# Eight modulation chunks moved from the WKV stage into the feed-forward stage, four of them on VectorE

## The chip, the cores and the metric

One Trainium2 chip, one of its cores. The metric is the device time of one execution in microseconds; the kernel before has a median of 1135.08 us over 3 runs (1134.55 to 1142.41). Lower is better.

## The reference, cut to what matters

Two blocks follow each other on 256 tokens of width 1024. The first block is a mixer (an attention branch and an RWKV-7 branch, merged under gates) and a gated feed-forward network of width 2816. The second is a state-space mixer and a mixture of 32 experts. What the change moves belongs to the second block but needs nothing of the first: the modulation, a product of one row with a matrix.

```python
# second_block; c is (1, 1024), w_ada is (1024, 6144)
mod = jax.nn.silu(c) @ w_ada[layer] + b_ada[layer]
sh1, sc1, g1, sh2, sc2, g2 = jnp.split(mod, 6, axis=-1)
h = modulate(x, sh1, sc1)          # first use: the input of the second block
...
x = x + g1[:, None, :] * mix
# first_block, the stage that receives the work
f = (jax.nn.silu(h @ w_ffn_gate[l]) * (h @ w_ffn_up[l])) @ w_ffn_down[l]
```

## The kernel before, in words

The program is written out by hand, one instruction stream for each engine, joined by semaphores. Each stream is executed in the order in which it is written, the DMA-issuing stream of SyncE (SP) among them.

**Weights.** All weights up to the experts pass through a ring of three slots of 4096 words per partition (2 MB each). The list `W` gives their order. SP walks it: before it fills a slot it waits (`consumed`) until the last matmul on the slot's former content is done. The keys that matter here: `("gate", 0..3)`, `("ada", c)` for the 512-column chunks of `w_ada`, and `("ff", 0..10)`, each of which holds 256 columns of `w_ffn_gate` and 256 of `w_ffn_up` (two DMAs of 1 MB). The content of most slots is split into a rounded high part (ScalarE, `high_parts`, L1645, two instructions of 128x2048) and a remainder (VectorE, `low_parts`, L558, two more); the matmuls are then three per product (`by_parts`, L767 to L769).

**PSUM.** `plan_banks` lists all uses of the eight banks in PE's order; use n goes to bank n mod 8 and waits until use n-8 has been drained (`write`, `drained`, `free`).

**One modulation chunk**, before: PE multiplies the chunk's eight k-tiles (128x512) by the broadcast column of silu(c), as four column tiles of 32 that run side by side (`ada_chunk`, L933); ScalarE copies the bank to `modp` (`ada_rows`, L1759); PE sums the four parts over the partitions with a constant (`ada_sum`, L911 into columns for chunks 0 to 3, L914 over rows for the gates 4, 5, 10, 11); VectorE adds the bias (`ada_sum`, L2316, L2319). Eight chunks, `ADA_EARLY`, are done in the WKV stage: `ada(turn)` stands between its steps and does the sum of the last chunk and the product of the next. Four others, `ADA_LATE`, are done in the second block and are not touched.

**The WKV stage** (146 to 220 us) inverts triangular 64x64 blocks level by level. At each of the levels 1 to 5, PE computes four groups `x` (L1018), which ScalarE copies (L1776); then, after `ada(lv + 1)`, four pairs of groups `d` and `dt` (L1018 too), which VectorE merges (L2345, L2347), and from these come the `x` of the next level. The chunks' DMAs, and those of gate 1 to 3, are `PACED`: a quarter at a time, each behind an event of the stage.

**The feed-forward stage** (317 to 442 us): 22 tiles f of 128 columns. PE makes gate and up of a tile in one bank (48 matmuls), ScalarE takes the silu (L1833), VectorE multiplies (L2451), and after each odd f ScalarE copies the pair's high part (L1838). Also after each odd f, both split slot `("ff", f // 2 + 3)`: the slot that SP requested when PE had finished this same f. The normed input `xn1`, in the arena, is dead once its transposes `("hT", 1, kk)` are drained.

Of the kernel before, what the change touches and what calls it, by code (L numbers as in the profile page):

```python
# [167 lines left out]
def ada_banks(turn):  # L168

    return ([("as", ADA_EARLY[turn - 1])] if turn else []) + ([("ad", ADA_EARLY[turn])] if turn < len(ADA_EARLY) else [])  # L170


def plan_banks():
# [32 lines left out]
    o += [("ff", m) for m in range(KF)]  # L206
# [21 lines left out]
ADA_EARLY = (0, 1, 2, 3, 4, 5, 10, 11)  # L228
ADA_LATE = (6, 7, 8, 9)
# [19 lines left out]
    ("modp", 2 * 512, TOKENS, GATES), ("gm", NT * HEADS * 4 * CH, WKV, WKV), ("dd", NT * HEADS * CH, WKV, WKV),  # L249
# [43 lines left out]
    "osb": 28672, "kk": 28672, "fpost": 28672, "ysq": 28672, "one": 28672, "acT": 29184, "modp": 29696, "xn1": 29696,  # L293
# [18 lines left out]
def build(nc, A, out):  # L312
    BANK = plan_banks()
    ctx = ExitStack()
    with ctx:
# [56 lines left out]
        def B(name, *dims):  # L372
# [6 lines left out]
            if len(dims) == 3:  # L379
# [14 lines left out]
        modp = {c: (junk[:, 512 * (c % 2):512 * (c % 2) + 512] if c in ADA_LATE else B("modp", 2)[:, c % 2])  # L394
                for c in ADA_EARLY + ADA_LATE}
# [83 lines left out]

        for c in ADA_EARLY:  # L480
            modulation(c)
# [24 lines left out]

        def level_paces(lv):
            nxt = ("x", 1, lv + 1, 0) if lv < LEVELS - 1 else ("w1", 1, 0)
            return ("dt", 0, lv, 1), ("dt", 1, lv, 1), nxt

        PACED = {("ada", ADA_EARLY[3]): (("g", 0, 0, 0), ("g", 0, 1, 0), ("g", 1, 0, 0)),
                 ("ada", ADA_EARLY[4]): (("n", 0, 0), ("n", 1, 0), ("x", 0, 1, 0)),
                 ("ada", ADA_EARLY[5]): level_paces(1), ("ada", ADA_EARLY[6]): level_paces(2),
                 ("ada", ADA_EARLY[7]): level_paces(3), ("gate", 1): level_paces(4), ("gate", 2): level_paces(5),
# [192 lines left out]
        def _(pe):  # L707
# [209 lines left out]
            def ada(turn):  # L917

                if turn:
                    ada_sum(ADA_EARLY[turn - 1])  # L920
# [1963 lines left out]
```

## Time and profile before

| what | us |
|---|---|
| median of 3 runs | 1135.08 |
| the profiled execution | 1133.99 |
| its span, first to last instruction | 1132.1 |
| mean granted TensorE clock | 0.991 of 2.4 GHz |
| WKV stage (from the first gram to the head means) | 145 to 219 |
| feed-forward tiles on PE | 317 to 442 |
| experts | from about 670 |

The table's stages are read from the timeline. Time outside the span is 1.9 us, and the profiled execution is 1.1 us under the median, so a difference of a few us counts from 1134.0.

### The profile page before, as it was taken

How to read it: one execution, taken by the hardware profiler on the slowest of the kernel's cores; microseconds unless marked ns; L12 is line 12 of the kernel's file. 1: busy time of each engine (PE TensorE's matmuls, PEld its weight loads, DVE VectorE, ACT ScalarE, POOL GpSimd, SP SyncE). 2: the span in 40 equal slices, each digit the busy share in tenths (PEclk: the TensorE clock that was granted, in tenths of full speed). 3: DMA queues.
4: the chain of work that ended last, by engine and by line, in shares of the span. 5: the costliest groups of instructions: out<-in, count | busy, mean ns of one | idle time of the engine just before them, and what ended most of it. 6: DMA issues, size and time to landing. Idle time of an engine off the chain costs nothing.

```text
span 1132.1 us, 17911 instructions
## 1 busy us (share of the span) xinstructions
PE 1058.2 (93%) x7545; PEld 720.2 (64%) x7545; DVE 461.8 (41%) x698; ACT 354.1 (31%) x508; POOL 39.5 (3%) x32
## 2 busy tenths in 40 slices
PE   5999999999999999999999999999899989898986
PEld 4997877799789999877986453444244433242432
DVE  4784244367655353557648351222122212121212
ACT  4752322364454343455543220111011111010102
POOL 0001310001000101000000000000000000000000
PEclk9999999999999999999989999999999999999999
DMA  9444377434545655463465869999999999999994
GB/s 318 147 174 159 135 236 238 139 145 173 187 130 183 190 186 186 186 219 130 167 224 209 363 257 421 419 419 421 420 421 421 420 421 421 421 420 421 420 420 191
DMA packets 95445, 316.31 MB, mean 279 GB/s; under 512 B 8262, under 2 KB 33174, under 8 KB 70678
## 3 DMA queue, kind: packets, MB, share of 16 engines
q1 hardware_dynamic: 94342, 312.70, 72.1%
q10 hardware_dynamic: 1040, 2.69, 0.7%
q8 instruction: 50, 0.82, 0.3%
q14 instruction: 13, 0.11, 0.0%
HBM read 314.32 MB, written 1.05 MB: 279 GB/s over the span
## 4 chain that ended last, share of the span: by engine, by line
PE 72%; DMA 21%; DVE 4%; ACT 2%; issue 1%; SPq 0%; POOL 0%; DVEq 0%; ACTq 0%
DMA arena<-in_w 20%; PE bank L1474 11%; PE bank L767 11%; PE bank L769 11%; PE bank L768 11%; PE bank L1498 4%; PE bank L753 4%; PE bank L1018 3%; PE bank L933 2%; PE bank L1454 1%; PE bank L967 1%; PE bank L744 1%; PE bank L1511 1%; PE bank L714 1%; DVE arena L2560 1%
## 5 line engine op out<-in xcount | busy, mean ns | idle before, releaser
L1474 PE MATMUL bank<-ring,hT 128*64 128x512 f32 x512 | 227.0, 595 | 29.8 <-DMA arena<-in_w 28.6
L1474 PE MATMUL bank<-arena,hT 128*64 128x512 f32 x512 | 227.0, 595 | 0.0
L769 PE MATMUL bank<-h_high,ring_low 128*128 128x256 f32 x688 | 193.8, 282 | 0.0
L1474 PEld LDWEIGHTS bank<-ring,hT 128*64 128x64 f32 x512 | 67.8, 137 | 182.2 <-issue 130.2
L558 DVE TENSOR_TENSOR ring_low<-ring,hi_high 128x2048 fp32r<-128x2048 f32 (+2 forms) x58 | 126.0, 2218 | 100.8 <-ACT hi_high L1645 100.8
L767 PE MATMUL bank<-h_high,hi_high 128*128 128x256 f32 x528 | 148.1, 280 | 0.0
L768 PE MATMUL bank<-h_low,hi_high 128*128 128x256 f32 x528 | 147.5, 279 | 0.0
L1645 ACT ACTIVATE hi_high<-ring 128x2048 fp32r<-128x2048 f32 (+2 forms) x58 | 104.5, 1854 | 92.0 <-DMA ring<-in_w_ffn_up 33.9
L769 PEld LDWEIGHTS bank<-h_high,ring_low 128*128 128x128 f32 x688 | 130.8, 190 | 0.0
L1498 PE MATMUL bank<-arena 128*64 128x512 f32 x384 | 113.3, 595 | 7.1 <-DVE hT L2772 6.7
L2778 DVE TENSOR_TENSOR arena<-arena,bank 128x512 f32<-128x512 f32 x16 | 17.4, 1084 | 231.0 <-ACT arena L2002 231.0
L767 PEld LDWEIGHTS bank<-h_high,hi_high 128*128 128x128 f32 x528 | 99.4, 188 | 1.1 <-issue 1.0
L768 PEld LDWEIGHTS bank<-h_low,hi_high 128*128 128x128 f32 x528 | 99.8, 189 | 0.1
L2002 ACT ACTIVATE arena<-bank 128x512 f32<-128x512 f32 x16 | 9.6, 598 | 232.8 <-PE bank L1474 232.8
L1474 PEld LDWEIGHTS bank<-arena,hT 128*64 128x64 f32 x512 | 67.8, 137 | 0.0
L1498 PEld LDWEIGHTS bank<-arena 128*64 128x64 f32 x384 | 35.1, 137 | 40.5 <-issue 39.4
L1498 PE MATMUL bank<-ring,arena 128*64 128x512 f32 x128 | 56.6, 595 | 4.3 <-ACT arena L2006 4.3
L2011 ACT ACTIVATE y_high<-con 128x512 fp32r<-128x512 f32 x32 | 20.2, 630 | 125.1 <-DVE con L2792 125.1
L2792 DVE SCALAR_TENSOR_TENSOR con<-bank,small,arena 128x512 f32<-128x512 f32 x32 | 24.0, 751 | 86.3 <-PE bank L1498 86.3
L767 PE MATMUL bank<-h_high,hrw_high 128*128 128x256 f32 x160 | 46.5, 291 | 0.7 <-DVE ring_low L558 0.7
L768 PE MATMUL bank<-h_low,hrw_high 128*128 128x256 f32 x160 | 45.9, 287 | 0.0
L1498 PEld LDWEIGHTS bank<-ring,arena 128*64 128x64 f32 x128 | 16.9, 137 | 37.7 <-issue 36.1
(401 smaller groups left out, 1706.7 us busy)
## 6 DMA issues: line engine op xcount, KB each, us to landing
arena<-in_w SPq DMA_DIRECT2D x112, 1024.0 KB, 23.0
ring<-in_w SPq DMA_DIRECT2D x80, 1024.0 KB, 20.5
ring<-in_w_in SPq DMA_DIRECT2D x12, 2048.0 KB, 7.8
ring<-in_w_ada SPq DMA_DIRECT2D x7, 2048.0 KB, 8.2
ring<-in_w_ffn_gate SPq DMA_DIRECT2D x11, 1024.0 KB, 5.5
ring<-in_w_ffn_up SPq DMA_DIRECT2D x11, 1024.0 KB, 8.2
ring<-in_w_ada SPq DMA_DIRECT2D x20, 512.0 KB, 5.0
ring<-in_w_ffn_down SPq DMA_DIRECT2D x5, 2048.0 KB, 7.9
```

The source lines that it names most:

```text
L558: return eng.tensor_tensor(ring_lo[:, r, c0:c1], ring[:, r, c0:c1], high_of(n)[:, c0:c1].bitcast(F32), ALU.subtract)
L753: last = mm(ps[:, 0:512], lhs[k][:, i * P:(i + 1) * P], w[:, k, 0:512], start=(k == 0), stop=(k == nk - 1))
L767: mm(ps, a[0], b[0], start=start, stop=False)
L768: mm(ps, a[0], b[1], start=False, stop=False)
L769: return mm(ps, a[1], b[0], start=False, stop=stop)
L933: last = mm(ps[32 * j:32 * j + 32, 0:512], cb[:, k, :], w[:, k, :], start=(kk == 0), stop=(kk == 1))
L1018: last = mm(ps[r, j * w:(j + 1) * w], left(4 * q + j, r), right(4 * q + j, r), start=True, stop=True)
L1474: last = mm(both(6 + half, x), hg[:, k, (2 * q + x) * CAP:(2 * q + x + 1) * CAP], w13s[x][k // 4][:, k % 4, half * EF:(half + 1) * EF], st ...
L1498: last = mm(both(4 + n, x), acT[:, 0, f, x * CAP:(x + 1) * CAP], w2s[q][x][f // 2][:, f % 2, n * 512:(n + 1) * 512], start=(f == 0), stop= ...
L1645: A_(high_of(n)[:, f], ring[:, r, f], ACT.Copy).then_inc(S("high"), 1)
L2011: A_(y_hi[n], y_out[:, n, :], ACT.Copy).then_inc(S("y_high"), 1)
L2792: V.scalar_tensor_tensor(y_out[:, n, :], bank[4 + n][:, :], slot_gate[:, 0:1], g2[:, n * 512:(n + 1) * 512], ALU.mult, ALU.mult).then_inc( ...
```

## The change

The eight early chunks leave the ring's list, the WKV stage and its banks. Gate 1 to 3 follow gate 0 directly and are loaded whole. The third and fourth attention output (`("o", 2)`) gets two idle matmuls (`keep_busy`) in place of `ada(0)`.

In the feed-forward stage, chunk t of the eight is tied to tiles f = 2t+2 and 2t+3. SP loads it in two halves of four k-tiles (1 MB) into one buffer, `ada_half`, which is the dead `xn1`: after slot `("ff", t + 3)` the first half, once the chunk before is consumed; then a wait for `half_used`; then the second half; only then slot `("ff", t + 4)`. Odd t go through PE as before, one half after each tile (`ada_part`), with the row copy on ScalarE ahead of its slot split. Even t (`ADA_DVE`) go through VectorE: per k-tile one product that accumulates in `modp` (`ada_products`, four after each tile, ahead of the slot split), and PE sums over the partitions with a constant of minus ones, which the bias addition takes back as a subtraction. The column sums of chunk t-1 stand behind tile 2t+3.

```diff
-    ("modp", 2 * 512, TOKENS, GATES), ("gm", ...
+    ("gm", ...
+ADA_DVE = ADA_EARLY[0::2]
+    for f in range(KF):
+        t = f // 2 - 1
+        o += [("ff", f)] + ([("as", ADA_EARLY[t - 1])] if f % 2 and 0 < t <= len(ADA_EARLY) else [])
+        o += [("ad", ADA_EARLY[t])] if f % 2 == 0 and 0 <= t < len(ADA_EARLY) and ADA_EARLY[t] not in ADA_DVE else []
+        ada_half = B("xn1").rearrange("p (k c) -> p k c", k=KD // 2)
@@ SP
-        for c in ADA_EARLY:
-            modulation(c)
-                if key == ("ada", 3):
+                if key == ("gate", 2):
...
+                if key[0] == "ff" and 3 <= key[1] < 3 + len(ADA_EARLY):
+                    c = ADA_EARLY[key[1] - 3]
+                    src = cols(A["w_ada_2"][0], c * 512, c * 512 + 512)
+                    if key[1] == 3:
+                        drained(sp, ("hT", 1, 3))
+                    elif ADA_EARLY[key[1] - 4] in ADA_DVE:
+                        sp.wait_ge(S("ada_acc"), ADA_DVE.index(ADA_EARLY[key[1] - 4]) + 1)
+                    else:
+                        filled(sp, ("ad", ADA_EARLY[key[1] - 4]))
+                    sp.dma_start(ada_half, src[:, 0:4, :]).then_inc(S("half_full"), 16)
+                    sp.wait_ge(S("half_used"), key[1] - 2)
+                    sp.dma_start(ada_half, src[:, 4:8, :]).then_inc(S("half_full"), 16)
@@ PE
                 if p == 2:
-                    ada(0)
+                    keep_busy(write(pe, ("o", p)), 2)
...
-                ada(lv + 1)
...
+            def ada_part(t, part):
+                c = ADA_EARLY[t]
+                pe.wait_ge(S("half_full"), 16 * (2 * t + part + 1))
+                if part == 0:
+                    pe.wait_ge(S("cb"), 1)
+                    ps = write(pe, ("ad", c))
+                else:
+                    ps = bank[BANK["ad", c][0]]
+                for j in range(4):
+                    last = mm(ps[32 * j:32 * j + 32, 0:512], cb[:, 4 * part + j, :], ada_half[:, j, :], start=(part == 0),
+                              stop=(part == 1), skip_group_check=True)
+                if part == 0:
+                    last.then_inc(S("half_used"), 1)
+                else:
+                    last.then_inc(*full(("ad", c)))
                 last.then_inc(*full(("ff", f)))
+                t = f // 2 - 1
+                if f % 2 and 0 < t <= len(ADA_EARLY):
+                    ada_sum(ADA_EARLY[t - 1])
+                if 0 <= t < len(ADA_EARLY) and ADA_EARLY[t] not in ADA_DVE:
+                    ada_part(t, f % 2)
@@ ScalarE, after the copy of the tile pair's high part
+                    if 0 <= f // 2 - 1 < len(ADA_EARLY) and ADA_EARLY[f // 2 - 1] not in ADA_DVE:
+                        ada_rows(ADA_EARLY[f // 2 - 1])
                     high_parts(N_FF + f // 2 + 3)
@@ VectorE
+            def ada_products(t, part):
+                c, acc = ADA_EARLY[t], modp[ADA_EARLY[t]]
+                dve.wait_ge(S("half_full"), 16 * (2 * t + part + 1))
+                if part:
+                    dve.wait_ge(S("half_used"), t + 1)
+                for j in range(4):
+                    k = 4 * part + j
+                    if k == 0:
+                        ins = V.tensor_scalar(acc, ada_half[:, j, :], csil[:, k:k + 1], None, ALU.mult)
+                    else:
+                        ins = V.scalar_tensor_tensor(acc, ada_half[:, j, :], csil[:, k:k + 1], acc, ALU.mult, ALU.add)
+                    if j < 3:
+                        link(ins)
+                    else:
+                        ins.then_inc(S("ada_acc") if part else S("half_used"), 1)
...
                 V.tensor_tensor(fT[:, f, :], sil[:, f % 2, :], ps[:, SEQ:2 * SEQ], ALU.mult).then_inc(*free(("ff", f)))
+                if 0 <= f // 2 - 1 < len(ADA_EARLY) and ADA_EARLY[f // 2 - 1] in ADA_DVE:
+                    ada_products(f // 2 - 1, f % 2)
                 if f % 2:
                     low_parts(N_FF + f // 2 + 3)
+                if f % 2 and 0 < f // 2 - 1 <= len(ADA_EARLY):
+                    ada_sum(ADA_EARLY[f // 2 - 2])
```

PE in the WKV stage at level 2, before: the last `x` group, the sum (L911), the chunk (L933), the first `d` group.

```order
L1018 MATMUL bank<-arena 64x64 [waits bank_free5,bank_free1,bank_free0]
L1018 MATMUL bank<-arena 64x64 x7
L911 MATMUL bank<-con,arena 128x1 [waits bank_free6,bank_free1]
L911 MATMUL bank<-con,arena 128x1 x3
L933 MATMUL bank<-ring,arena 32x512 [waits bank_free7,cb,slot_full2]
L933 MATMUL bank<-ring,arena 32x512 x7
L1018 MATMUL bank<-arena 64x64 [waits bank_free0,bank_free2]
```

The same place now (L1026 is the former L1018):

```order
L1026 MATMUL bank<-arena 64x64 [waits bank_free0,bank_free4,bank_free3]
L1026 MATMUL bank<-arena 64x64 x7
L1026 MATMUL bank<-arena 64x64 [waits bank_free1,bank_free5]
L1026 MATMUL bank<-arena 64x64 x7
L1026 MATMUL bank<-arena 64x64 [waits bank_free2]
```

The `d` groups now follow the `x` groups directly.

SP in the feed-forward stage, before: two DMAs for each slot, behind one wait for PE.

```order
L638 DMA ring<-in_w_ffn_gate 128x8x256 [waits bank_full4]
L638 DMA ring<-in_w_ffn_up 128x8x256
L638 DMA ring<-in_w_ffn_gate 128x8x256 [waits bank_full6]
L638 DMA ring<-in_w_ffn_up 128x8x256
```

SP now, from slot 3 to slot 5 (L619 is the former L638; L629 and L631 are the halves of chunks 0 and 1):

```order
L619 DMA ring<-in_w_ffn_gate 128x8x256 [waits bank_full4]
L619 DMA ring<-in_w_ffn_up 128x8x256
L629 DMA arena<-in_w_ada 128x4x512 [waits bank_free2]
L631 DMA arena<-in_w_ada 128x4x512 [waits half_used]
L619 DMA ring<-in_w_ffn_gate 128x8x256 [waits bank_full6]
L619 DMA ring<-in_w_ffn_up 128x8x256
L629 DMA arena<-in_w_ada 128x4x512 [waits ada_acc]
L631 DMA arena<-in_w_ada 128x4x512 [waits half_used]
L619 DMA ring<-in_w_ffn_gate 128x8x256 [waits bank_full1]
```

Each slot now stands behind a wait for the consumer of a half, and each chunk's first half behind the consumer of the chunk before.

VectorE in the feed-forward stage now, tiles 1 to 4 (L2467 is the tile's product, the former L2451; L545 the slot split, the former L558; L2336 and L2338 the new products of chunk 0):

```order
L2467 TENSOR_TENSOR arena<-arena,bank 128x256 [waits sil,bank_full4]
L545 TENSOR_TENSOR ring_low<-ring,hi_high_51 128x2048 [waits high] x2
L2467 TENSOR_TENSOR arena<-arena,bank 128x256 [waits sil,bank_full5]
L2336 TENSOR_SCALAR arena<-arena,small 128x512 [waits half_full]
L2338 SCALAR_TENSOR_TENSOR arena<-arena,small 128x512 [waits dve_step] x3
L2467 TENSOR_TENSOR arena<-arena,bank 128x256 [waits sil,bank_full6]
L2338 SCALAR_TENSOR_TENSOR arena<-arena,small 128x512 [waits half_used,half_full]
L2338 SCALAR_TENSOR_TENSOR arena<-arena,small 128x512 [waits dve_step] x3
L545 TENSOR_TENSOR ring_low<-ring,hi_high_49 128x2048 [waits high] x2
L2467 TENSOR_TENSOR arena<-arena,bank 128x256 [waits sil,bank_full7]
```

Before, the same stretch held the tiles' products and the splits alone; the products of chunk 0 now stand between the split of slot 3 and the split of slot 4.

## Rows read from the trace of the kernel before

**Rows 1.** The page: busy time, share of the span, instructions; chain by engine.

```profile
PE 1058.2 (93%) x7545; PEld 720.2 (64%) x7545; DVE 461.8 (41%) x698; ACT 354.1 (31%) x508; POOL 39.5 (3%) x32
...
PE 72%; DMA 21%; DVE 4%; ACT 2%; issue 1%; SPq 0%; POOL 0%; DVEq 0%; ACTq 0%
```

**Rows 2.** Stretches: PE, PEld, DVE, ACT, POOL busy (x), clock, DMA share, GB/s.

```profile
156.00:206.00 50.00, 48.40 (x1087) 36.67 (x1087) 18.55 (x42) 13.59 (x34) 0.00 (x0) 1.00 0.80 253
...
330.00:442.00 112.00, 112.00 (x954) 112.00 (x952) 44.93 (x37) 44.51 (x48) 12.85 (x10) 1.00 0.56 179
```

**Rows 3.** Timeline, WKV level 2 to 3: start, length, engine, line; idle before.

```profile
165.87 1.05 PE L911 MATMUL bank<-con,arena 128*128 128x1 f32 x8
166.86 1.92 PE L933 MATMUL bank<-ring,arena 128*32 128x512 f32 x16
168.71 5.81 PE L1018 MATMUL bank<-arena 64*64 64x64 f32 x192
...
172.71 0.44 DVE L2347 COPY_PREDICATED arena<-lvl,bank 128x256 f32<-128x256 uint8 x1
...
173.17 1.78 ACT L1776 ACTIVATE arena<-bank 128x256 f32<-128x256 f32 x4 [3.73 <-PE bank L1018]
```

**Rows 4.** Timeline, the WKV stage's start and end.

```profile
143.50 0.66 PE L988 MATMUL bank<-arena 128*64 128x256 f32 x4 [0.88 <-POOL arena L2074]
...
146.26 4.87 DVE L2328 TENSOR_TENSOR arena<-bank,con 128x512 f32<-128x512 f32 x8 [6.10 <-PE bank L1008]
...
151.50 2.08 PE L1018 MATMUL bank<-con,arena 64*64 64x64 f32 x64
...
154.63 0.44 DVE L2338 COPY_PREDICATED arena<-lvl,arena 128x256 f32<-128x256 uint8 x1
...
155.78 1.05 PE L911 MATMUL bank<-con,arena 128*128 128x1 f32 x8
...
205.78 1.12 PE L914 MATMUL bank<-arena,con 128*128 128x512 f32 x2
```

**Rows 5.** Timeline, feed-forward stage: SP, ScalarE, VectorE.

```profile
329.71 0.37 SPq L638 DMA_DIRECT2D ring<-in_w_ffn_gate  x1
...
341.02 0.37 SPq L638 DMA_DIRECT2D ring<-in_w_ffn_gate  x1
...
338.61 3.73 ACT L1645 ACTIVATE hi_high<-ring 128x2048 fp32r<-128x2048 f32 x2 [7.26 <-DMA ring<-in_w_ffn_up]
...
350.76 3.72 ACT L1645 ACTIVATE hi_high<-ring 128x2048 fp32r<-128x2048 f32 x2 [4.32 <-DMA ring<-in_w_ffn_up]
...
340.56 4.49 DVE L558 TENSOR_TENSOR ring_low<-ring,hi_high 128x2048 fp32r<-128x2048 f32 x2 [9.93 <-ACT hi_high L1645]
344.97 0.74 DVE L2451 TENSOR_TENSOR arena<-arena,bank 128x256 f32<-128x256 f32 x2
```

**Rows 6.** DMA issues: count, KB each, median us to landing.

```profile
ring<-in_w_ffn_gate SPq DMA_DIRECT2D x11, 1024.0 KB, 5.5
ring<-in_w_ffn_up SPq DMA_DIRECT2D x11, 1024.0 KB, 8.2
...
xres<-in_x SPq DMA_DIRECT2D x1, 1024.0 KB, 5.3
```

**Rows 7.** Instructions by shape, VectorE: busy us, mean ns.

```profile
L2124 DVE TENSOR_SCALAR arena<-xres,small 128x1024 f32<-128x1024 f32 x4 | 2.8, 749 | 0.1
...
L2259 DVE SCALAR_TENSOR_TENSOR arena<-arena,parcol 128x256 f32<-128x256 f32 x4 | 1.7, 473 | 0.0
L2242 DVE SCALAR_TENSOR_TENSOR arena<-arena 128x1024 f32<-128x1024 f32 x1 | 1.2, 1226 | 0.0
```

**Rows 8.** Stretches of 2 us around PE's wait at 312 us; columns as in rows 2.

```profile
312.00:314.00 2.00, 0.61 (x2) 0.00 (x0) 1.00 (x3) 0.77 (x3) 0.00 (x0) 1.00 1.08 350
314.00:316.00 2.00, 1.52 (x10) 1.33 (x11) 0.76 (x2) 0.60 (x2) 0.00 (x0) 0.92 0.95 305
316.00:318.00 2.00, 2.00 (x11) 1.77 (x10) 1.67 (x5) 2.00 (x7) 0.00 (x0) 0.50 0.03 10
318.00:320.00 2.00, 2.00 (x15) 2.00 (x15) 1.56 (x4) 2.00 (x3) 0.00 (x0) 0.73 0.00 0
```

More of the change, by code:

```diff
@@ L505, in build @@
         SLOTS, loads = {}, [0] * RING
[L507 to L514, printed above, removed]
-                 ("gate", 3): (("u", 0, 0), ("u", 0, 1), ("u", 1, 0))}
         for n, (key, parts, last) in enumerate(W):
-            loads[n % RING] += 16 * (4 if key in PACED else len(parts))
+            loads[n % RING] += 16 * len(parts)
             SLOTS[key] = (n % RING, loads[n % RING])
@@ L900, in ada_sum @@
             def ada_sum(c):
-                drained(pe, ("ad", c))
+                one = K("thirty_second")
+                if c in ADA_DVE:
+                    one = K("neg_ones")
+                    pe.wait_ge(S("ada_acc"), ADA_DVE.index(c) + 1)
+                else:
+                    drained(pe, ("ad", c))
                 ps = write(pe, ("as", c))
@@ L906, in ada_sum @@
                     for k in range(KD):
-                        last = mm(ps[o:o + 64, k:k + 1], modp[c][:, 64 * k:64 * k + 64], K("thirty_second")[:, 0:1],
+                        last = mm(ps[o:o + 64, k:k + 1], modp[c][:, 64 * k:64 * k + 64], one[:, 0:1],
                                   start=True, stop=True)
@@ L910, in ada_sum @@
                     for j in range(4):
-                        last = mm(ps[:, j:j + 1], modp[c][:, j * P:(j + 1) * P], K("thirty_second")[:, 0:1],
+                        last = mm(ps[:, j:j + 1], modp[c][:, j * P:(j + 1) * P], one[:, 0:1],
                                   start=True, stop=True)
                 else:
-                    last = mm(ps[:, 0:512], K("thirty_second"), modp[c], start=True, stop=True)
+                    last = mm(ps[:, 0:512], one, modp[c], start=True, stop=True)
                 last.then_inc(*full(("as", c)))
-            def ada(turn):
-                if turn:
-                    ada_sum(ADA_EARLY[turn - 1])
-                if turn < len(ADA_EARLY):
-                    ada_chunk(ADA_EARLY[turn])
+            def ada_part(t, part):
[13 more added lines that the diff above has]
+                    last.then_inc(*full(("ad", c)))
             def ada_chunk(c):
@@ L1022, in _ @@
                 grams(i, q)
-            ada(1)
             for i, q in both:
@@ L1047, in _ @@
                 group(("w1", i, q), q, lambda h, r: gm[r, i, h, 2 * CH:3 * CH], lambda h, r: vp[r, i, h, :])
-            ada(LEVELS + 1)
             for i, q in both:
@@ L1052, in _ @@
                 group(("u", i, q), q, lambda h, r: ddT[r, i, h, :], lambda h, r: zb[r, i, h, :], P)
-            ada(LEVELS + 2)
             def at(p):
@@ L2339, in _ @@
             for lv in range(1, LEVELS):
-                ada_sum(ADA_EARLY[lv])
                 for i, q in both:
@@ L2382, in _ @@
             state_out(2)
-            for c in (2, 3):
-                drained(dve, ("as", c))
-            V.tensor_scalar(modc[:, 8:16], modc[:, 8:16], 1.0, None, ALU.add).then_inc(S("mod"), 1)
             for i in range(NT):
```

45 lines of the change are left out of this document (16 added, 29 removed).

## The prediction

> **What bounds the kernel now.** I read the page's busy line and its chain first: PE is busy 93% of the span and is 72% of the chain that ended last, DMA 21% [rows 1]. Then I asked stretch by stretch, because the change takes work out of one stage and puts it into another. In the WKV stage between 156 and 206 us PE is busy 48.4 of 50 us; in the feed-forward stage it is busy all of 112 us, at full clock, while VectorE and ScalarE are busy 45 us each and DMA moves 179 GB/s [rows 2]. So both stages are PE's, and PE time removed from the first is worth something only if no chain of ScalarE and VectorE stands behind it; PE time added to the second counts in full, and anything that PE waits for there is new time.
>
> The row that decides is a different one. In the feed-forward stage VectorE has much idle time, but it runs late. SP asks for slot 3 at 329.71, which is PE's end of tile 1. ScalarE starts its split at 338.61, VectorE ends it at 340.56 + 4.49 = 345.05, and only then comes VectorE's product of tile 2, at 344.97 [rows 5]. Tile 2 itself ended at 329.71 + 5.65 = 335.36 on PE (the slots are asked for every 341.02 - 329.71 = 11.31 us, two tiles, 5.65 us each). VectorE is therefore 9.6 us behind PE, and costs nothing, since nobody waits for it. The change makes SP wait for it, and PE for SP.
>
> I sum against the profiled execution, 1133.99 us; the median shown is 1.1 us above it.
>
> **Taken out of the WKV stage.** At level 2 the sum runs from 165.87 and the chunk from 166.86, and the next group starts at 168.71: 2.84 us [rows 3]. Is a wait behind it? Four `x` groups and eight `d`/`dt` groups take PE 5.81 us in one piece, 0.48 us each. VectorE's last merge of the level ends at 172.71 + 0.44 = 173.15, and the `x` group that needs it, the last of four, starts at 168.71 + 11 x 0.48 = 174.0. ScalarE copies one `x` group in 0.45 us, as fast as PE makes them; its first copy is at 173.17, just behind the first group, and the last `d` pair, which needs the fourth copy at 174.95, stands 6 groups later. So PE stays the limit without the filler and all of the 2.84 is saved. There are six such places (levels 1 to 5 and behind `w1`): three with column sums at 2.84, three with row sums, 1.06 (205.78 to 206.84) instead of 0.99, at 2.91: 17.3 us. The last sum alone gives 1.06 [rows 4].
>
> The place behind the grams is worth less. Its 2.84 us ended at 151.50, but VectorE's gram copies last until 146.26 + 4.87 = 151.13, and its eight predicated copies, which now end at 154.63 + 0.44 = 155.07, need 2.8 us after that: 153.9. The last `x` group follows and ends at 154.4, against 155.8 now [rows 4]: 1.4 us saved. Sum: 17.3 + 1.06 + 1.4 = **19.7 us**. What is next there is VectorE, 0.9 us behind PE at every level. Bounds: 0, if every filler only covered a wait, and 21.2, all of PE's work; the rows put it at the upper end.
>
> **Edits that I cost at nothing.** `ada(0)` becomes four rows of idle matmul; PE waits for POOL until 143.50 either way (0.88 us of idle time now) [rows 4]. Gate 1 to 3 and the router's small loads come earlier by tens of us, in a stage whose DMA is lightly used, and gate 1 is used only after the WKV stage; were it late, PE would stand there. The row copies and sums that leave ScalarE and VectorE in the WKV stage lie in their idle time. ScalarE's row copies in the feed-forward stage (four, 0.6 us, ahead of a split) lie in the 9 us in which it waits for the slot anyway. Fewer banks are left for the tiles: a tile now waits for the bank of four to five tiles back, 22 us, and VectorE is behind by less.
>
> **Added to the feed-forward stage: PE's work.** A half chunk is 8 of the 16 rows of 1.92 us, 1.0 us; eight halves (four chunks) 7.7. Eight sums, four of 0.99 and four of 1.06: 8.2 [rows 3, 4]. Together 16 us, all on the path: even without a wait this returns most of the 19.7.
>
> **Added: the wait for the halves.** VectorE's accumulating product on 128x512, from and to SBUF, isn't in the trace: 473 ns at 256 columns and 1226 at 1024 bound it; on the line between them it is 0.72, and with its link to the next 0.75. The one plain product, half of the 749 ns and some fixed time, 0.45 [rows 7]. So a chunk's first half costs VectorE 0.45 + 3 x 0.75 = 2.7 us, its second 3.0. One DMA of 1 MB lands in 5.3 us, a second one behind it 2.7 us later (8.2 against 5.5) [rows 6].
>
> Follow chunk 0 (VectorE) and 1 (PE). First half of 0: there early. VectorE's product of tile 2 ends at 345.34, its four chunk products at 348.05. SP asks for the second half then, not before: 353.35. Four more products: 356.35. Only now does SP ask for the first half of chunk 1: 361.65. PE wants it after tile 4, at 341.02 + 5.65 = 346.67. **It waits 15.0 us**, and queued behind that matmul are all later tiles.
>
> Does this come again? From the arrival of one odd chunk's first half to the next: half chunk 1.0, tile 5.65, then SP may ask for the next slot; slot until ScalarE starts 9.3 (338.61 - 329.71 = 8.9, 350.76 - 341.02 = 9.7); split 345.05 - 338.61 = 6.45; tile product 0.4; first products 2.7; load 5.3; second products 3.0; load 5.3 [rows 5 to 7]. That is 39.1 us for four tiles, which take 22.6 us now. It is a closed loop with every engine in series, so the slack that PE's wait gives to the others is used up each time. Odd chunks are 1, 3, 5, 7: the first wait 15.0, three turns of 39.1 - 22.6 = 16.5 (PE's added 4.1 us of each turn are inside), 49.5, the work of the last turn 4.1, and VectorE's bias additions in the loop, 0.15 twice and 0.69 once, 1.0. Together 69.6.
>
> **The clock.** After 1.4 us of idle time in 312 to 314 us PE's granted clock is 0.92, 0.50 and 0.73 in the next three stretches of 2 us, so 1.2 GHz for about 3.4 us of time, which loses 0.16 + 1.0 + 0.54 = 1.7 us of work [rows 8]. A wait of 12 to 15 us should do at least that, and the work behind it (half chunk, tile) is in the loop: 4 x 1.7 = 6.8 us.
>
> The Trainium skill, page "TensorE: Matmul & The Clock Gate", section "HAM oscillation — how this bites in real kernels", describes this very pattern as a reason against waiting for each transfer: every wait that is long enough puts the clock back to half, and the price is paid at each. By that rule, the trace agrees with it once; without it the sum would be 6.8 us less.
>
> **Order of loads.** In the sum the second half of an even chunk lands in 5.3 us although SP puts the next slot's 2 MB right behind it. Nothing in the rows excludes that the three share the engines and all end together: then 2.7 to 5.4 us more for each such half, at most 4 x 5.4 = 22 us. I take 5.3, because gate lands in 5.5 with up right behind it, as a lone load does [rows 6].
>
> The Trainium skill, page "DMA: Bandwidth & Descriptors", section "Queues, rings and completion order", says that each DMA engine takes the descriptors of one issuing queue in ring order, so an earlier load isn't slowed by a later one of the same queue. The rows agree; without the rule up to 22 us would be added.
>
> **Sum:** 1133.99 - 19.7 + 69.6 + 6.8 = **1190.7**, so 1191 us.
>
> **Rivals.**
> 1. *The halves arrive in time.* If VectorE did its products at the pace of PE's tiles, each half would have 5.65 us for 5.3 us of load, and PE would never wait: 1134.0 - 19.7 + 16 = 1130, no change that can be told. For it: VectorE is idle 60% of the stage. Against: its lateness is order, not load; the split stands ahead of the tile product in its stream, and SP's request behind it. It decides as long as VectorE is less than about 1 us behind PE; the row says 9.6 [rows 5]. 5%.
> 2. *It happens once.* The first wait lets the splits run ahead and later halves are in time: 1134.0 - 19.7 + 16 + 15.0 + 1.7 = 1147. Against: SP may ask for a slot only after PE's tile, and the loop above starts anew at each. 7%.
> 3. *The WKV stage gives nothing back*, since the fillers covered waits: 1191 + 19.7 = 1210. For it: ScalarE and VectorE do alternate with PE there. Against: rows 3, as worked out. 6%.
>
> **How the numbers follow.** Forecast 82%. Its own bounds: the VectorE product at 0.47 or 1.23 takes 8 us off or adds 13 over four turns; loads at 4.9 to 8 add up to 22; the clock loses nothing (-7) or twice as much (+7). All of one sign at once is unlikely: 1172 to 1212, which leaves rivals 1 and 2 out and takes rival 3 in. A measurement of this kernel can tell about 1% from no change. Slower by over 1%: forecast, 2 and 3, 95%; within 1%: rival 1, 4%; faster by over 1%: 1%.
>
> **What would show it.** In the profile after: PE between 156 and 206 us without L911 and L933, the levels 5.8 us apart instead of 8.7; the head means near 199 us. In the feed-forward stage four idle times of PE ahead of the half chunk's first matmul, released by a DMA of w_ada, the first about 15 us and the others about 12, four tiles 39 us apart, a clock of 0.5 behind each; VectorE idle twice per even chunk for a half. SP's slot requests in pairs at unequal distance. After the stage nothing but a shift. I am wrong if PE's waits there are short or single (rivals 1, 2), or if the levels' pitch stays above 7 us (rival 3).

## The result, and the profile after

The changed kernel takes 1191.04 us (median of 4 runs, 1184.88 to 1193.89) against 1134.82 us for the kernel before on the same chip: ratio 1.0474, 95% interval 1.0412 to 1.0535. It is slower by 56 us; 1191 was forecast. The profiled execution took 1191.4 us, so the accounts below explain 1191.4 - 1134.0 = 57.4 us.

The page of the kernel after, PE's busy line and its granted clock in 40 slices of 30 us (compare [rows 1]):

```profile
PE 1062.6 (89%) x7485; PEld 725.2 (61%) x7485; DVE 484.1 (41%) x730; ACT 352.6 (30%) x504; POOL 39.5 (3%) x32
...
PEclk9999999999977987999998999999999999999999
```

PE is busy for only 4.4 us more, in a span that is 57.4 us longer: the loss isn't added work as such but time in which PE stands. The clock's string says where: slices 12 to 16, which are 327 to 476 us. PE's waits name it:

```profile
PE bank L925 <- DMA arena<-in_w_ada: 52.9, 4, 14.7
PE bank L1483 <- DMA arena<-in_w: 28.5, 23, 1.3
PE bank L1507 <- DVE hT L2796: 6.6, 7, 1.0
```

The first line (total, times, longest) is new: four waits, 52.9 us, each ahead of an odd chunk's first half. The experts' waits in the second line were 28.6 us before: in the experts nothing changed but the time of day. These are the four waits on PE's timeline (start, length, idle time before in brackets):

```profile
338.28 1.93 PE L925 MATMUL bank<-arena 128*32 128x512 f32 x8 [14.67 <-DMA arena<-in_w_ada]
...
378.97 1.94 PE L925 MATMUL bank<-arena 128*32 128x512 f32 x8 [11.78 <-DMA arena<-in_w_ada]
...
420.76 1.94 PE L925 MATMUL bank<-arena 128*32 128x512 f32 x8 [12.74 <-DMA arena<-in_w_ada]
...
463.22 1.93 PE L925 MATMUL bank<-arena 128*32 128x512 f32 x8 [13.69 <-DMA arena<-in_w_ada]
```

From one to the next are 40.7, 41.8 and 42.5 us for four tiles, which took 22.6 before. One turn of this loop can be read on SP's queue (time of issue; L619 is a slot, L629 a first half, L631 a second half):

```profile
324.54 0.37 SPq L631 DMA_DIRECT2D arena<-in_w_ada  x1
324.95 0.51 SPq L619 DMA_DIRECT2D ring<-in_w_ffn_gate  x1
...
332.73 0.37 SPq L629 DMA_DIRECT2D arena<-in_w_ada  x1
340.28 0.37 SPq L631 DMA_DIRECT2D arena<-in_w_ada  x1
347.11 0.37 SPq L619 DMA_DIRECT2D ring<-in_w_ffn_gate  x1
...
365.01 0.37 SPq L631 DMA_DIRECT2D arena<-in_w_ada  x1
...
373.43 0.37 SPq L629 DMA_DIRECT2D arena<-in_w_ada  x1
```

and on VectorE and ScalarE, which lie between SP's entries:

```profile
329.58 3.12 DVE L2338 SCALAR_TENSOR_TENSOR arena<-arena,small 128x512 f32<-128x512 f32 x4 [4.74 <-DMA arena<-in_w_ada]
...
357.33 4.49 DVE L545 TENSOR_TENSOR ring_low<-ring,hi_high 128x2048 fp32r<-128x2048 f32 x2 [9.31 <-ACT hi_high L1654]
...
362.14 0.48 DVE L2336 TENSOR_SCALAR arena<-arena,small 128x512 f32<-128x512 f32 x1
362.65 2.33 DVE L2338 SCALAR_TENSOR_TENSOR arena<-arena,small 128x512 f32<-128x512 f32 x3
```

```profile
355.38 3.72 ACT L1654 ACTIVATE hi_high<-ring 128x2048 fp32r<-128x2048 f32 x2 [5.85 <-DMA ring<-in_w_ffn_up]
```

Put together, from the first wait's end to the second's, with the forecast beside it:

| step of the loop | read from | us | forecast |
|---|---|---|---|
| half chunk and tile on PE | 338.28 to 347.11 | 8.8 | 6.65 + 1.7 clock |
| slot requested until ScalarE splits it | to 355.38 | 8.3 | 9.3 |
| split, tile product, first chunk products | to 365.01 | 9.6 | 9.55 |
| second half lands, second products | to 373.43 | 8.4 | 8.3 |
| next first half lands | to 378.97 | 5.5 | 5.3 |
| sum | | 40.7 | 40.8 |

In the next two turns the slot took 9.1 and 9.6 us and the other steps changed little, which makes 41.8 and 42.5. In the last, VectorE's bias addition over 512 columns (0.68 us) stands in the chain as well.

In the WKV stage PE runs almost without a pause. Its timeline from the grams to the end of the levels:

```profile
141.81 0.66 PE L996 MATMUL bank<-arena 128*64 128x256 f32 x4 [0.79 <-POOL arena L2080]
...
150.22 20.78 PE L1026 MATMUL bank<-arena 64*64 64x64 f32 x672
171.36 12.00 PE L1026 MATMUL bank<-arena 64*64 64x64 f32 x350 [0.36 <-issue]
...
196.44 1.97 PE L1153 MATMUL bank<-arena,con 128*128 128x256 f32 x8 [0.68 <-ACT arena L1795]
```

The second of these is the answer to [rows 3]: 672 matmuls in one piece, where before a sum and a chunk of 2.84 us stood in each level. No wait took their place (the pauses between such pieces are 0.4 to 0.5 us), so they had covered none. The head means, at 218.85 us before (its L1149), stand at 196.44. A part of the gain is lost again behind the levels: PE pauses for 1.00 us at 185.9, and the granted clock then falls, which it didn't before (1.00 in all of 206 to 220 us):

```profile
188.00:190.00 2.00, 2.00 (x65) 2.00 (x61) 1.21 (x5) 0.38 (x1) 0.00 (x0) 0.71 0.00 0
190.00:192.00 2.00, 2.00 (x46) 2.00 (x43) 0.18 (x1) 0.01 (x1) 0.00 (x0) 0.50 0.03 8
192.00:194.00 2.00, 2.00 (x82) 2.00 (x81) 0.24 (x1) 0.38 (x1) 0.00 (x0) 0.94 0.00 0
```

PE is busy in all of these 6 us and loses 0.58 + 1.0 + 0.12 = 1.7 us of them.

The account of the 57.4 us, by the same event in both traces:

| from, to | after - before, us |
|---|---|
| up to the WKV stage: PE's clock is 1.00 after, 0.83 before in 50 to 60 us | -1.7 |
| grams to head means, with 1.7 of clock given back inside | -20.7 |
| head means to SP's request of slot 3 (306.69, before 329.71) | -0.6 |
| from there to the request behind tile 19 (486.26, before 431.47) | +77.8 |
| the last sum, behind it | +1.1 |
| the rest; a clock gap in the second block is deeper after | +1.6 |

The first and the last of these aren't the change's doing by anything that the trace shows; they nearly cancel. The last: PE is busy throughout in both traces, and the granted clock falls to 0.50 at 576 to 588 us before (3.4 us lost) and at 632 to 644 after (5.1). The first, stretches of 10 us, before and after (columns as in [rows 2]):

```profile
50.00:60.00 10.00, 10.00 (x64) 9.35 (x63) 6.90 (x11) 5.93 (x6) 0.40 (x1) 0.83 0.50 170
```

```profile
50.00:60.00 10.00, 10.00 (x76) 9.35 (x75) 6.91 (x11) 5.94 (x6) 0.40 (x1) 1.00 0.52 188
```

### The profile page after: what moved, and what is told of

The parts are those of the page before. It is cut to its first block, busy times and chain, and to the rows that moved or that the text cites. A ratio compares the mean times of both kernels' runs of the same rounds, so it can differ in the third digit from the quotient of the medians.

```text
span 1189.5 us, 17803 instructions
## 1 busy us (share of the span) xinstructions
PE 1062.6 (89%) x7485; PEld 725.2 (61%) x7485; DVE 484.1 (41%) x730; ACT 352.6 (30%) x504; POOL 39.5 (3%) x32
## 4 chain that ended last, share of the span: by engine, by line
PE 62%; DMA 26%; DVE 7%; ACT 2%; issue 1%; SPq 0%; POOL 0%; DVEq 0%; ACTq 0%
DMA arena<-in_w 19%; PE bank L1483 11%; PE bank L760 9%; PE bank L762 9%; PE bank L761 9%; PE bank L1507 4%; DMA arena<-in_w_ada 4%; PE bank L746 4%; PE bank L1026 3%; DMA ring<-in_w_ffn_up 3%; DVE ring_low L545 2%; DVE arena L2338 2%; PE bank L1463 1%; PE bank L975 1%; PE bank L737 1%
## 5 line engine op out<-in xcount | busy, mean ns | idle before, releaser
L1483 PE MATMUL bank<-ring,hT 128*64 128x512 f32 x512 | 226.9, 595 | 29.8 <-DMA arena<-in_w 28.5
L1483 PE MATMUL bank<-arena,hT 128*64 128x512 f32 x512 | 226.9, 595 | 0.0
L1483 PEld LDWEIGHTS bank<-ring,hT 128*64 128x64 f32 x512 | 67.8, 137 | 182.2 <-issue 130.5
L545 DVE TENSOR_TENSOR ring_low<-ring,hi_high 128x2048 fp32r<-128x2048 f32 (+2 forms) x58 | 125.8, 2215 | 110.3 <-ACT hi_high L1654 110.3
L760 PE MATMUL bank<-h_high,hi_high 128*128 128x256 f32 x528 | 153.7, 291 | 0.7 <-DVE h_low L2156 0.7
L761 PE MATMUL bank<-h_low,hi_high 128*128 128x256 f32 x528 | 150.5, 285 | 0.0
L1654 ACT ACTIVATE hi_high<-ring 128x2048 fp32r<-128x2048 f32 (+2 forms) x58 | 104.4, 1854 | 130.3 <-DMA ring<-in_w_ffn_up 71.1
L1507 PE MATMUL bank<-arena 128*64 128x512 f32 x384 | 113.3, 595 | 7.1 <-DVE hT L2796 6.6
L1483 PEld LDWEIGHTS bank<-arena,hT 128*64 128x64 f32 x512 | 67.9, 137 | 0.0
L1507 PE MATMUL bank<-ring,arena 128*64 128x512 f32 x128 | 56.6, 595 | 4.3 <-ACT arena L2012 4.3
L1507 PEld LDWEIGHTS bank<-arena 128*64 128x64 f32 x384 | 35.1, 137 | 40.5 <-issue 39.4
L925 PE MATMUL bank<-arena 128*32 128x512 f32 x64 | 12.0, 832 | 52.9 <-DMA arena<-in_w_ada 52.9
L2017 ACT ACTIVATE y_high<-con 128x512 fp32r<-128x512 f32 x32 | 20.2, 630 | 125.1 <-DVE con L2816 125.1
```

Source lines behind the costliest of these rows:

```text
L545: return eng.tensor_tensor(ring_lo[:, r, c0:c1], ring[:, r, c0:c1], high_of(n)[:, c0:c1].bitcast(F32), ALU.subtract)
L760: mm(ps, a[0], b[0], start=start, stop=False)
L761: mm(ps, a[0], b[1], start=False, stop=False)
L1483: last = mm(both(6 + half, x), hg[:, k, (2 * q + x) * CAP:(2 * q + x + 1) * CAP], w13s[x][k // 4][:, k % 4, half * EF:(half + 1) * EF], st ...
L1507: last = mm(both(4 + n, x), acT[:, 0, f, x * CAP:(x + 1) * CAP], w2s[q][x][f // 2][:, f % 2, n * 512:(n + 1) * 512], start=(f == 0), stop= ...
L1654: A_(high_of(n)[:, f], ring[:, r, f], ACT.Copy).then_inc(S("high"), 1)
```

## The experiments

The theory is that of the prediction: the stage is a closed chain PE, slot, split, VectorE's products, half, half, PE, which one buffer and the place of the split close; the clock comes on top. The rivals that the runs were to tell apart: (A) VectorE has too much work; (B) only the loads' bandwidth counts; and whether the WKV stage gave back what was forecast, or the stage lost less. "Stage" below is the time from SP's request of slot 3 to that of slot 11, the first `down` slot (behind tile 17): 90.45 us before (329.71 to 420.16), 166.0 after (306.69 to 472.71). Each experiment is an edit of the changed kernel.

**One part alone: the WKV stage without the chunks.**

```diff
-        o += [("ff", f)] + ([("as", ADA_EARLY[t - 1])] if ... else [])
-        o += [("ad", ADA_EARLY[t])] if ... else []
+        o += [("ff", f)]
@@ and in each stream: no halves, no ada_part, ada_products, ada_rows or ada_sum of the eight
+            link(V.tensor_copy(modc[:, 0:16], par("b_ada_2", 0, 16)))
```

> The changed kernel with the eight early chunks left out altogether (no loads, products or sums; shift, scale and gates of the second block's mixer are the bias alone). It is the WKV half of the change by itself. My theory: PE's fillers there cost what they took, so 1134 - 20.7 = about 1113 us, with the feed-forward tiles at 5.65 us each and no wait of PE between them. Rival (the fillers only covered waits of the level chain): the same as before, 1130 to 1135. If the rest of the program depends on where the chunks stood (banks, slots), the time lies under 1110 or the later stages differ.

Measured: 1112.27 us (1111.04 to 1113.87) against 1136.99, ratio 0.9786 (0.9768 to 0.9804). The stage is exactly 90.45 us again. Shift, scale and gates are the bias alone here. So the removal is worth 1.0 - 0.9786 = 2.1%, 24 us; from the grams to the head means this trace is 21.7 us shorter than before, the trace of after 20.7. The feed-forward stage has to answer for the rest, a loss of about 80 us.

**The work without the loads.** Only the first half is loaded; nothing waits for another.

```diff
                     if key[1] == 3:
                         drained(sp, ("hT", 1, 3))
-                    elif ...
-                    sp.dma_start(ada_half, src[:, 0:4, :]).then_inc(S("half_full"), 16)
-                    sp.wait_ge(S("half_used"), key[1] - 2)
-                    sp.dma_start(ada_half, src[:, 4:8, :]).then_inc(S("half_full"), 16)
+                        sp.dma_start(ada_half, src[:, 0:4, :]).then_inc(S("half_full"), 16)
@@ PE and VectorE
-                ...wait_ge(S("half_full"), 16 * (2 * t + part + 1))
+                ...wait_ge(S("half_full"), 16)
```

> The changed kernel with all its new instructions on PE, VectorE and ScalarE, but of the 16 half loads only the first is made; all halves read it (so the modulation is computed from the wrong rows), and SP has no wait for a consumer. My theory: the new work alone costs PE's 16 us against the first experiment, 1113 + 16 = 1129 us, no wait of PE above 1 us in the feed-forward stage. Rival A (VectorE's products are too much for it, and PE waits for the splits): above 1145 us, with waits of PE released by VectorE's split. Rival B (the work costs more than 16 us because small matmuls between tiles are slow): 1135 to 1145.

Measured: 2364.51 us, which says nothing on the question: the modulation is another, and the kernel takes its other, longer branch for the experts (PE's lines L1570 and L1585 in place of L1483 and L1507). I had not foreseen this. The stage ends before the experts and can be read: 306.52 to 411.49, 104.97 us, 14.5 more than before, and in 270 to 520 us PE waits for no half:

```profile
PE bank L754 <- issue: 3.2, 2, 1.6
PE bank L713 <- DVE arena L2124: 1.9, 2, 1.5
```

With 3.1 us of halves' and sums' work behind tile 17 this is 17.6 us of added work of PE, where the sum had 16. VectorE did all its products here and held nobody up: rival (A) falls.

**All eight chunks on PE.**

```diff
-ADA_DVE = ADA_EARLY[0::2]
+ADA_DVE = ()
```

> The changed kernel with no chunk on VectorE (all eight on PE by halves), loads as they are. My theory: VectorE's lateness drops out of the loop, but each first half is still asked for behind a slot of 2 MB, right after the chunk before: eight waits of 3 to 5 us instead of four of 12 to 15, 29 us, PE's work 24 us: 1134 - 21 + 24 + 29 = 1166 us, up to 1180 if each of these waits also halves the clock. Rival (DMA bandwidth sets the waits, 4 MB per pair of tiles): unchanged at 1185 to 1195. Rival (VectorE alone is the cause): no waits, 1137 us.

Measured: 1186.39 us (1184.74 to 1189.49), ratio 1.043 (1.0411 to 1.045). The stage is 161.1 us. This expectation was missed, by 6 us at its upper end. PE's waits came nearly as expected, eight instead of four and shorter (32.9 us where 29 were expected):

```profile
PE bank L925 <- DMA arena<-in_w_ada: 32.9, 8, 5.4
```

What the expectation had only at its upper end, the clock, stands in the stretches of 2 us about one of them (clock in the third column from the end):

```profile
340.00:342.00 2.00, 0.64 (x4) 0.20 (x8) 1.40 (x1) 2.00 (x2) 0.00 (x0) 0.50 0.18 67
...
344.00:346.00 2.00, 2.00 (x12) 2.00 (x11) 1.42 (x2) 0.00 (x0) 0.00 (x0) 0.50 0.77 169
```

The wait is 4.4 us, and yet the granted clock behind it is 0.50, the lower of the two levels. Read in stretches of 1 us, PE's busy time in the stage times what the granted clock is below 1.00 makes 15.0 us of lost work, and 8.8 in the kernel after. So 20.0 us less of waits stand against 6.2 more of clock and 9 more of chunk work: waits a third as long and twice as many returned only 5 us. The clock fell behind seven of the eight; behind this one it stayed at 1.00 in all stretches from 398 to 408 us:

```profile
402.87 1.06 PE L925 MATMUL bank<-arena 128*32 128x512 f32 x8 [3.47 <-DMA arena<-in_w_ada]
```

**The split behind the next tile.** This takes ScalarE's and VectorE's split out of the chain from the tile to the products.

```diff
                 A_(sil[:, f % 2, :], ps[:, 0:SEQ], ACT.Silu).then_inc(S("sil"), 1)
+                if f and f % 2 == 0:
+                    high_parts(N_FF + f // 2 + 2)
                 if f % 2:
...
-                    high_parts(N_FF + f // 2 + 3)
@@ VectorE, low_parts, in the same way
```

> The changed kernel with one move: ScalarE and VectorE split a slot one tile later, behind the product of the next even tile, so that VectorE's product of that tile, and the chunk products behind it, no longer stand behind the split. No work is added or removed. My theory: VectorE's first four products start at the tile's end instead of some 9 us later, the loop gets about 4 us shorter per turn, waits of PE 11 and three of 8 us instead of 15 and three of 12 to 14: 1134 - 21 + 57 = 1170 us. Rival (the lateness costs nothing, the loads alone make the wait): 1185 to 1195.

Measured: 1179.65 us (1175.11 to 1180.85), ratio 1.0363 (1.0336 to 1.0389); the stage is 155.6 us, 10.4 less than after, where about 17 were expected. This expectation was missed by 10 us. The waits are still four, and 40.7 us where 35 were expected; the clock costs 10.5 us of the stage, counted as in the run before:

```profile
PE bank L925 <- DMA arena<-in_w_ada: 40.7, 4, 12.3
```

VectorE's timeline shows what is late next:

```profile
318.61 0.49 DVE L2337 TENSOR_SCALAR arena<-arena,small 128x512 f32<-128x512 f32 x1 [5.50 <-DMA arena<-in_w_ada]
...
326.60 4.00 DVE L2339 SCALAR_TENSOR_TENSOR arena<-arena,small 128x512 f32<-128x512 f32 x4 [0.40 <-DMA arena<-in_w_ada]
```

Now VectorE is early enough to wait for the first half itself, which lands at 318.6, behind the slot's 2 MB that were asked for at 306.44. So the order of the split is a part of the chain (10 us), not the whole of it.

**PE kept busy in the waits**, to tell the clock's share.

```diff
                 c = ADA_EARLY[t]
+                if part == 0:
+                    keep_busy(write(pe, ("ad", c)), 15 if t == 1 else 12)
                 pe.wait_ge(S("half_full"), 16 * (2 * t + part + 1))
```

> The changed kernel with idle matmuls (128x512 fp32, the kernel's own keep_busy) in each of PE's four waits: 15 ahead of the first, 12 ahead of the others, so that PE runs until about the time the half lands. Nothing else. My theory of the clock term: the wait itself stays (PE idles 0 to 2 us instead of 12 to 15), but the half chunk and the tile behind it run at 2.4 GHz, 2.2 us less per turn, so 4 x 2.2 = 9 us less than the changed kernel: 1182 us, granted clock 1.0 in the stage. Rival (the half clock costs nothing, since the loop is bound by loads and VectorE): 1189 to 1193. If the idle matmuls overrun the half's landing, the time is above that by the overrun.

Measured: 1184.63 us (1183.53 to 1188.11), ratio 1.0445 (1.0418 to 1.0471), an interval that lies within that of the kernel after. The stage is 162.0 us: 4.0 less than after, where 9 were expected. PE's idle time ahead of the halves is 8.3 us in all, and the first half chunk takes 1.07 us instead of 1.93:

```profile
338.19 1.07 PE L927 MATMUL bank<-arena 128*32 128x512 f32 x8 [2.18 <-DMA arena<-in_w_ada]
```

SP's next slot request comes at 345.22, so half chunk and tile take 7.0 us instead of 8.8, and the clock's 1.8 us are shown. At the other three waits the edit did not do what it was made for. Half chunk and tile take 8.5 us there (8.46, 8.49, 8.49), for the granted clock falls in the tile behind the half chunk, although PE has stood for only 2 us behind 10.46 us of idle matmuls:

```profile
378.00:380.00 2.00, 2.00 (x14) 1.37 (x7) 2.00 (x2) 0.85 (x2) 0.00 (x0) 0.61 0.24 23
380.00:382.00 2.00, 2.00 (x12) 2.00 (x11) 1.71 (x3) 0.00 (x0) 0.00 (x0) 0.54 0.77 266
```

Counted over the stage, the clock still costs 5.1 us, 3.7 less than after, and the stage is 4.0 shorter: what the clock gave back the stage gained, and the other 5 us were never given back.

**Two buffers.** The second halves go into the last four tiles' place of `fT` and `fh`, which is unused until tile 18, and each half has a semaphore of its own. SP's order becomes slot, second half of the last chunk, first half of the next.

```diff
-        ada_half = B("xn1").rearrange("p (k c) -> p k c", k=KD // 2)
+        ada_first = B("xn1").rearrange("p (k c) -> p k c", k=KD // 2)
+        tail = [... tiles 18 to 21 of n ... for n in ("fT", "fh")]
...
+                if 0 < t <= len(ADA_EARLY):
+                    if t > 1:
+                        load_half(t - 1, 1)
+                    if t < len(ADA_EARLY):
+                        load_half(t, 0)
```

> The changed kernel with a buffer for each half: the first halves stay in the dead normed input, the second ones go to the last four tiles' places in the feed-forward's own output (high and low part, written only from tile 18 on). SP asks for the first half of chunk t+1 as soon as the first half of t is used, the second likewise, each behind at most one slot. VectorE is as late as before. My theory: two of the loop's loads leave it, VectorE's lateness stays: waits of 6 us and three of 4, 1134 - 21 + 40 = 1153 us. Rival (the single buffer was not the cause, the lateness alone): 1170 or more. Rival (the buffer alone was): below 1135.

Measured: 1159.4 us (1158.17 to 1160.8), ratio 1.0229 (1.0201 to 1.0257), 6 us above what was expected. The waits fall from 52.9 to 20.0 us, the clock's share stays (9.0 us in the stage):

```profile
PE bank L942 <- DMA arena<-in_w_ada: 20.0, 5, 5.8
```

Not one byte less is loaded, and the stage is 32.7 us shorter (133.3). Rival (B), bandwidth, falls: what was missing is a place to load into, and with it the freedom to ask earlier (the edit changes both, and chunk 0 is asked for one slot earlier).

**Two buffers and the split behind the next tile**, the two edits above together.

> Two buffers as in the run before, and the slot split one tile later on ScalarE and VectorE. My theory: both legs of the loop are gone, each half is asked for 5 us or more ahead of its need, PE does not wait for halves; what is left is its work: 1134 - 21 + 16 = 1129 us. Rival (bandwidth: 4 MB in 12.3 us, or the split now comes too late for the tiles): waits of PE released by VectorE's split or by a half, 1135 to 1160.

Measured: 1130.48 us (10 runs, 1128.68 to 1132.02), ratio 0.9961 (0.9945 to 0.9977). No wait for a half is left; PE is busy in all of 300 to 410 us, at full clock:

```profile
300.00:410.00 110.00, 110.00 (x901) 102.32 (x900) 72.84 (x73) 44.15 (x46) 12.32 (x8) 1.00 0.89 298
```

In the kernel after PE is busy for 127.12 of 180 us there, at a clock of 0.84:

```profile
300.00:480.00 180.00, 127.12 (x973) 114.27 (x972) 74.47 (x78) 50.12 (x52) 11.51 (x9) 0.84 0.58 193
```

The stage is 105.4 us, 15 more than before, as in the run without loads. Alone, the late split gained 10 us of stage and the buffers 33; together they gain 61: as long as one of them closes the chain, part of what the other frees is given back. The time is also that of rival 1 of the prediction, 1130, now that the halves are in time.

The stage of each kernel divides into PE's idle time, the work lost to the half clock (stretches of 1 us) and the rest:

| kernel | stage, us | PE idle | clock | rest |
|---|---|---|---|---|
| after | 166.0 | 52.9 | 8.8 | 104.3 |
| all on PE | 161.1 | 32.9 | 15.0 | 113.2 |
| late split | 155.6 | 40.7 | 10.5 | 104.4 |
| PE kept busy (44.4 of idle matmuls taken off) | 117.6 | 8.3 | 5.1 | 104.2 |
| two buffers | 133.3 | 19.6 | 9.0 | 104.7 |
| two buffers, late split | 105.4 | 0 | 0 | 105.4 |
| no loads | 105.0 | 0 | 0 | 105.0 |

All but "all on PE" give PE the same work, and their rest is the same to about 1 us: waits and clock are the whole difference.

**And all eight chunks on VectorE.** PE then has the sums alone.

```diff
-ADA_DVE = ADA_EARLY[0::2]
+ADA_DVE = ADA_EARLY
```

> As the run before, with all eight chunks on VectorE, so that PE adds only the sums, 8 us. VectorE has then 11.5 us of work in 12.3 us of each tile pair. My theory: 1134 - 21 + 8 = 1121 us if VectorE keeps up. Rival (VectorE falls behind, being slowed by POOL's remainders or by late halves, and PE waits for splits): 1130 to 1150.

Measured: 1122.36 us (1121.38 to 1127.22), ratio 0.9913 (0.988 to 0.9946), and on another chip:

> The version with two buffers, the late split and all eight chunks on VectorE once more, with more rounds, for its place against the kernel before. Expected from the first time: 1122 us, a ratio of 0.99, its interval clear of 1. Rival (the first figure was luck of the chip): a ratio whose interval holds 1.

Measured: 1122.52 us (6 runs, 1118.79 to 1125.93) against 1135.76 (11 runs), ratio 0.9878 (0.9848 to 0.9908). This version is faster than both kernels, on both chips with an interval clear of 1, though by only about 1% against the kernel before. Its stage is 99.0 us, 8.5 more than before: seven of the eight sums, and one wait of PE for VectorE of 0.8 us. VectorE now does what the idea promised, and is busy for 86% of the time:

```profile
300.00:410.00 110.00, 109.23 (x898) 107.58 (x897) 94.89 (x102) 43.46 (x45) 13.84 (x8) 1.00 0.94 305
```

**The row copies.** ScalarE's copy goes behind its split.

```diff
+                    high_parts(N_FF + f // 2 + 3)
                     if 0 <= f // 2 - 1 < len(ADA_EARLY) and ADA_EARLY[f // 2 - 1] not in ADA_DVE:
                         ada_rows(ADA_EARLY[f // 2 - 1])
-                    high_parts(N_FF + f // 2 + 3)
```

> The changed kernel with ScalarE's four row copies behind its slot split instead of ahead of it. My theory: the copy's only reader is PE's sum two tiles later, some 13 us on, and the split is 6 us, so the place of the copy decides nothing: the same as the changed kernel, 1184 to 1192 us. Rival (the copy's place matters, because the split is then 0.6 us earlier, or the bank is held longer): a change of more than 6 us either way.

Measured: 1193.3 us (1190.03 to 1194.93), ratio 1.0492 (1.0451 to 1.0533), where the kernel after has 1.0474 (1.0412 to 1.0535): no difference. That part of the change decides nothing.

## Why the prediction was right

1. **What bounds the kernel** stood: both stages are PE's. That VectorE's 9.6 us behind PE [rows 5] decide was said too strongly. They are one term of the loop: without them the stage is 10.4 us shorter, with a second buffer and VectorE as late as before 32.7, and only with both is there no wait.
2. **Taken out of the WKV stage, 19.7 us:** 20.7 measured, in parts that partly cancel. Behind the grams 1.5 us (1.4 forecast). From there to the end of the levels and the last sum 20.6 (18.4 forecast): 1.1 of the 2.2 more is a pause of PE ("issue", level 1) that stood in the trace of before; the rest wasn't followed. Behind it 1.3 us came back, where the clock fell (1.7). In the other kernels with the same WKV stage and no such fall, grams to head means are 20.2 to 22.5 us shorter than before.
3. **Edits costed at nothing:** `keep_busy` hides behind POOL (0.79 us of idle time behind it, 0.88 before). The place of the row copies was tried and costs nothing. The earlier loads of gate 1 to 3 and the fewer banks weren't tried alone, but there is no wait for either in PE's list.
4. **PE's added work, 16 us:** 14.5 and 14.9 up to tile 17 in the two kernels without waits, and 3.1 behind: 17.6 to 18.0, so about 2 too low.
5. **The wait for the halves.** First wait 15.0, measured 14.67. First products 2.7, measured 2.85 (321.67, where the plain one starts, to 322.19 + 2.33); second 3.0, measured 3.12. The line between 473 ns and 1226 ns [rows 7] gave 0.72 us at 512 columns, 0.75 with the link; the group's mean is 752 ns:

```profile
L2338 DVE SCALAR_TENSOR_TENSOR arena<-arena,small 128x512 f32<-128x512 f32 x28 | 21.0, 752 | 20.7 <-DMA arena<-in_w_ada 19.9
```

6. **The clock, 1.7 us at each wait:** mis-sized, and too low. Half chunk and tile behind a wait take 8.8, 9.0, 8.7 and 9.5 us where 6.65 is their time at full clock, so 2.0 to 2.8 us each; by the granted clock the four cost 8.8 us, where the sum had 6.8. Stretches of 2 us behind the first wait:

```profile
338.00:340.00 2.00, 1.72 (x8) 0.20 (x8) 2.00 (x2) 1.57 (x2) 0.00 (x0) 0.50 0.00 0
340.00:342.00 2.00, 2.00 (x12) 1.86 (x9) 2.00 (x2) 0.00 (x0) 0.00 (x0) 0.50 0.36 52
342.00:344.00 2.00, 2.00 (x18) 2.00 (x17) 0.35 (x2) 0.00 (x0) 0.00 (x0) 0.89 0.95 359
344.00:346.00 2.00, 2.00 (x20) 2.00 (x19) 0.00 (x0) 0.00 (x0) 0.00 (x0) 1.00 0.34 125
```

   In [rows 8] PE had started again before the clock fell; here it works at 0.50 from the first matmul on (0.86 + 1.0 + 0.22 = 2.1 us). The Trainium skill, page "TensorE: Matmul & The Clock Gate", section "HAM oscillation — how this bites in real kernels", says that the price is paid at every wait of the loop. This trace agrees at all four. With all chunks on PE, where the waits are 3.4 to 5.4 us, it was paid at seven of eight.
7. **Order of loads, 5.3 us taken and up to 22 more left open:** the second half of chunk 0 was asked for at 324.54, right ahead of a slot's 2 MB, and VectorE started on it at 329.58, 5.04 us later. The Trainium skill, page "DMA: Bandwidth & Descriptors", section "Queues, rings and completion order", has the rule that each DMA engine takes a queue's descriptors in ring order; the row agrees, and nothing of the 22 us came.
8. **Rivals.** 1 (halves in time) and 2 (once) fall by the four waits; 3 by 672 matmuls in one piece. All three were judged as they turned out. What rival 1 was said to need was too little, though: in the run with the late split VectorE keeps up with PE at tile 2, and PE still waits for 40.7 us, since the first half itself lands late behind the slot's 2 MB and the buffer is single. And the loop's three turns took 57.1 us more than twelve tiles did before, not 55.6 (49.5, 5.1 of clock and 1.0 of bias additions), and two unrelated clock gaps (-1.7 and +1.6) happen to cancel, as do the WKV stage's 1.0 and the feed-forward stage's 2.5 us in part: that the median hits 1191 to 0.1 us is luck, the terms are right to 1 or 2 us each.

**What stays open.** Why the slot takes 8.3 us in the first turn and 9.6 in the third; about 1 us of the WKV stage's gain; and why PE's added work is 2 us above the sum. Three expectations (all on PE, late split, two buffers) were 6 to 10 us too low: PE's waits came out 2 to 6 us longer than expected there, and the clock cost 9 to 15 us; why the waits were longer wasn't followed to its end.

## What to carry to other kernels

Before an in-order queue is made to wait for a consumer, look how far that consumer runs behind the engine that sets the time, not how idle it is: VectorE was idle for 60% of the stage and 9.6 us late, and that lateness was one of the steps that came round with each turn. Then walk once round from the load to its own next request; if the sum is longer than the work of one turn, a second buffer comes first and the order of the streams second, and neither is worth its full gain alone (33 and 10 us, together 61). And take work out of the bound engine altogether: with half of the chunks on PE the kernel was 4 us faster than before, with none of them 12 to 13.

## What the hardware showed unexpectedly

- VectorE's product on 128x512 isn't a constant. In the kernel with all chunks on it the mean is 881 ns instead of 752, and in the late-split kernel four took 4.00 us (row above) instead of 3.12. The slow ones lie beside POOL's instructions, which take 1.5 to 1.8 us there and 1.3 elsewhere. That each slows the other was seen, not tried.

```profile
L2356 DVE SCALAR_TENSOR_TENSOR arena<-arena,small 128x512 f32<-128x512 f32 x56 | 49.3, 881 | 1.7
```

- The granted clock falls within the wait, not at its end: PE stopped at 323.6 us, and the record has 1.00 up to 328 and 0.69 in the next stretch. Behind the four waits the work ran on below full clock for 4 to 5 us.

```profile
326.00:328.00 2.00, 0.00 (x0) 0.00 (x0) 0.00 (x0) 0.00 (x0) 0.91 (x1) 1.00 0.87 312
328.00:330.00 2.00, 0.00 (x0) 0.00 (x0) 0.41 (x1) 0.00 (x0) 0.00 (x0) 0.69 1.06 388
```

- The granted clock fell where PE had hardly paused: behind a pause of 1.0 us in the WKV stage, behind 2 us in the kernel whose PE is kept busy, and in the second block (632 to 644 us) with no pause at all. What decides it, these runs don't show.
